# Two-layer retention and sparse-attention step: only real token rows move through the experts, splitting reordered, one weight unit's low half on Pool

## What is computed

```python
def grouped_moe(h, w_router, b_router, w_gate, w_up, w_down):
...
    vals, idx = lax.top_k(jnp.where(in_grp, probs, -jnp.inf), TOPK_EXPERTS)
    wts = vals / jnp.sum(vals, -1, keepdims=True)
    gates = jnp.sum(jax.nn.one_hot(idx, N_EXPERTS, dtype=F32) * wts[..., None], axis=-2).astype(h.dtype)
    y = jnp.zeros_like(h)
    for e in range(N_EXPERTS):
        a = jax.nn.silu(h @ w_gate[e]) * (h @ w_up[e])
        y = y + gates[..., e:e + 1] * (a @ w_down[e])
    return y
```

## Time and profile before

| | before |
|---|---|
| median of 3 runs | 2274.32 us (2268.29 to 2278.16) |
| the profiled execution's own time | 2277.34 us |
| span of its trace | 2275.6 us |
| PE busy | 1903.2 us (84%) |
| DVE busy | 1089.5 us (48%) |
| ACT busy | 768.7 us (34%) |
| POOL busy | 239.6 us (11%) |
| moved by DMA | 412.19 MB, mean 181 GB/s |

### The profile page before, as it was taken

How to read it: one execution, slowest core, us unless ns; L and a number is a source line. 1 busy time by engine, 2 the same in 40 slices (tenths; PEclk the granted TensorE clock), 3 DMA queues, 4 the chain that set the end, 5 groups by cost and what they waited for, 6 DMA issues and landing times.

```text
span 2275.6 us, 20410 instructions
## 1 busy us (share of the span) xinstructions
PE 1903.2 (84%) x6689; PEld 1039.8 (46%) x6689; DVE 1089.5 (48%) x1674; ACT 768.7 (34%) x993; POOL 239.6 (11%) x235
## 2 busy tenths in 40 slices
PE   2899899999899997399999479996568972999990
PEld 0443323343233334187878134343343441877870
DVE  0320352210342017298988371126742173989886
ACT  0110211111211001388786211124442021888861
POOL 0000000000000000432221120000000003122201
PEclk8899999999999997699999789995775975999995
DMA  9232172423163124699998922021002233999983
GB/s 340 102 133 77 72 277 75 158 75 111 67 247 105 54 74 147 244 359 392 392 393 332 378 77 79 20 58 38 1 1 74 85 140 102 367 393 392 393 301 122
DMA packets 194993, 412.19 MB, mean 181 GB/s; under 512 B 14382, under 2 KB 18558, under 8 KB 194877
## 3 DMA queue, kind: packets, MB, share of 16 engines
q1 hardware_dynamic: 168962, 322.26, 39.5%
q0 software_dynamic: 21248, 72.02, 8.4%
q10 hardware_dynamic: 4712, 17.02, 2.1%
HBM read 363.36 MB, written 47.90 MB: 181 GB/s over the span
## 4 chain that ended last, share of the span: by engine, by line
PE 68%; DVE 11%; DMA 8%; issue 4%; DVEq 4%; ACT 3%; POOL 1%; POOLq 0%; ACTq 0%; SPq 0%
PE bank L586 34%; PE bank L884 17%; PE bank L579 3%; DMA RING<-in_w_mod 3%; PE bank L811 3%; DMA RING<-in_w_gate 3%; ACT WH L1319 2%; PE bank L796 2%; PE bank L977 1%; PE bank L785 1%; DVEq L2228 1%; PE bank L664 1%; POOL slot_d L1644 1%; DVE WL L2083 1%; PE bank L781 1%
## 5 line engine op out<-in xcount | busy, mean ns | idle before, releaser
L586 PE MATMUL bank<-RING,HT 128*128 128x512 f32 (+3 forms) x1600 | 685.8, 584 | 15.9 <-ACT HT L1146 13.3
L2083 DVE TENSOR_TENSOR WL<-RING,WH 128x2048 fp32r<-128x2048 f32 x192 | 436.7, 2293 | 81.1 <-ACT WH L1319 79.4
L586 PEld LDWEIGHTS bank<-RING,HT 128*128 128x128 f32 (+1 forms) x1600 | 263.8, 172 | 397.8 <-issue 377.5
L1319 ACT ACTIVATE WH<-RING 128x2048 fp32r<-128x2048 f32 x192 | 364.9, 1915 | 115.4 <-PE bank L884 92.4
L579 PE MATMUL bank<-cst,M 128*128 128x128 f32 (+3 forms) x721 | 114.2, 289 | 119.4 <-DMA M<-h_d,slot_c 71.8
L884 PE MATMUL bank<-WH,HGH 128*128 128x512 f32 x512 | 204.1, 399 | 3.0 <-DVE HGL L2094 3.0
L884 PE MATMUL bank<-WL,HGH 128*128 128x512 f32 x512 | 201.3, 393 | 0.0
L884 PE MATMUL bank<-WH,HGL 128*128 128x512 f32 x512 | 201.3, 393 | 0.0
L579 PEld LDWEIGHTS bank<-cst,M 128*128 128x128 f32 (+3 forms) x721 | 92.0, 156 | 178.3 <-DMA M<-h_d,slot_c 72.8
L586 PE MATMUL bank<-RING,M 128*128 128x512 f32 (+1 forms) x320 | 138.6, 593 | 0.3 <-ACT M L1268 0.3
L884 PE MATMUL bank<-WH,ATH 128*128 128x512 f32 x256 | 102.8, 402 | 14.4 <-DVE ATL L2110 14.4
(11 more groups left out here) (277 smaller groups left out, 2095.1 us busy)
## 6 DMA issues: line engine op xcount, KB each, us to landing
RING<-in_w_gate SPq DMA_DIRECT2D x64, 1024.0 KB, 12.1
RING<-in_w_up SPq DMA_DIRECT2D x64, 1024.0 KB
RING<-in_w_down SPq DMA_DIRECT2D x64, 1024.0 KB, 12.0
RING<-in_w_mod SPq DMA_DIRECT2D x24, 2048.0 KB, 9.5
RING<-in_w_in_ret SPq DMA_DIRECT2D x12, 2048.0 KB, 12.1
RING<-in_state_ret SPq DMA_DIRECT2D x16, 1024.0 KB, 8.6
out_ret_sample<-RING POOLq DMA_DIRECT2D x16, 1024.0 KB, 6.8
RING<-in_w_in_dsa SPq DMA_DIRECT2D x5, 2048.0 KB, 14.4
```

The costliest lines, as they stand in the source:

```text
L586: last = pe.matmul(out, lhs[:, k, :], w[:, k, :], start=start and k == 0, stop=stop and k == K - 1)
L1319: act.activation(WH[:, u % SPLIT, :, :], raw(u % RAW), ACT.Copy).then_inc(S("hi_rdy"), 1)
L2083: TT(WL[:, u % SPLIT, :, :], raw(u % RAW), WH[:, u % SPLIT, :, :].bitcast(F32), ALU.subtract)\
```

## The change

Token rows alone move: the table of slots is filled with 1,040 (a row that doesn't exist) in place of 0, tokens are numbered 0 to 1,039 (k * 520 + token for a token's first and second expert), `h_d` holds the rows twice, and the gather skips rows out of range. The store of an item becomes an indirect DMA to `y_d`, by the same numbers, that skips rows out of range too. So `y_d` holds 1,040 rows in token order, and the end of a layer reads them with plain DMAs. The clearing of part of `y_d` at the start goes.

Another order of splitting: `take_a(1)` stands ahead of unit 12 on ACT and on DVE, and both halves of `take_y` are ACT's. The low half of unit 10 (POOL_UNIT, the eleventh of each pair) is POOL's; DVE waits for it at u = 10 and passes the count on to `lo_rdy` with a copy of one column.

The core of the diff:

```diff
@@ constants
-    tok[:, :] = (np.arange(TILES) * P)[None, :] + i[:, None]
+    tok[:, :, :] = (np.arange(2) * TOK)[None, :, None] + (np.arange(TILES) * P)[None, None, :] + i[:, None, None]
@@ scalar: pair(i, end)
                     def take_y(j, u):
                         used(u)
                         act.wait_ge(S(f"y_st{j}"), (i + 1) * 16)
-                        act.activation(Y[j][:, NB:D], bank[5 + 2 * j][:, :], ACT.Copy).then_inc(S(f"y_ev_a{j}"), 1)
+                        for h in range(2):
+                            act.activation(Y[j][:, h * NB:(h + 1) * NB], bank[4 + 2 * j + h][:, :], ACT.Copy)\
+                                .then_inc(S(f"y_ev{j}"), 1)
                     for u in range(SPLIT, SPLIT + len(UNITS)):
+                        if u == 12:
+                            take_a(1)
                         if not end or u < len(UNITS):
                             high(i, u)
...
-                        if u == 12:
-                            take_a(1)
@@ gpsimd
-            pool.dma_start(y_items[:, NE:, :],
-                           zero_f.rearrange("p (o d) -> p o d", o=1).to_broadcast([P, ITEMS - NE, D])).then_inc(S("y_zero"), 16)
-            pool.dma_start(slot_d.rearrange("(p i) o -> p (i o)", p=P), zero_i[:, :]).then_inc(S("slot_zero"), 16)
+            def no_slots():
+                pool.dma_start(slot_d.rearrange("(p i) o -> p (i o)", p=P), none_i[:, :]).then_inc(S("slot_zero"), 16)
+            no_slots()
@@ gpsimd: experts(l)
-                    pool.dma_start(h_d[cols(t), :], HN[t % 2][0:rows(t), :]).then_inc(S(f"h_st{t % 2}"), 16)
+                    pool.dma_start(h_d.rearrange("(k t) d -> t k d", k=2)[cols(t)],
+                                   HN[t % 2][0:rows(t), :].rearrange("p (o d) -> p o d", o=1).to_broadcast([rows(t), 2, D]))\
+                        .then_inc(S(f"h_st{t % 2}"), 16)
...
                 pool.wait_ge(S("slots_in"), 16 * (l + 1))
+                if l == 0:
+                    no_slots()
...
-                                            in_offset=bass.IndirectOffsetOnAxis(ap=slot_c[:, j:j + 1], axis=0))\
+                                            in_offset=bass.IndirectOffsetOnAxis(ap=slot_c[:, j:j + 1], axis=0),
+                                            bounds_check=2 * TOK - 1, oob_is_err=False)\
...
                 def store(j, k):
-                    pool.wait_ge(S(f"y_ev_d{j}"), (first + k) + 2)
-                    pool.wait_ge(S(f"y_ev_a{j}"), (first + k) + 2)
-                    pool.dma_start(y_items[:, bass.ds(k * 2 + j, 1), :].rearrange("p o d -> p (o d)"), Y[j][:, :])\
+                    pool.wait_ge(S(f"y_ev{j}"), (first + k) * 2 + 4)
+                    nc.gpsimd.tensor_tensor(slot_o[:, j:j + 1], slot_i[:, bass.ds(k * 2 + j, 1)], zero_i[:, 0:1], ALU.add)
+                    pool.drain()
+                    pool.indirect_dma_start(out=y_d, out_offset=bass.IndirectOffsetOnAxis(ap=slot_o[:, j:j + 1], axis=0),
+                                            in_=Y[j][:, :], in_offset=None, bounds_check=2 * TOK - 1, oob_is_err=False)\
                         .then_inc(S(f"y_st{j}"), 16)
+                def low(k):
+                    pool.wait_ge(S("hi_rdy"), (first + k) * len(UNITS) + (POOL_UNIT + 1))
+                    nc.gpsimd.tensor_tensor(WL[:, POOL_UNIT % SPLIT, :, :], raw(POOL_UNIT % RAW),
+                                            WH[:, POOL_UNIT % SPLIT, :, :].bitcast(F32), ALU.subtract)\
+                        .then_inc(S("pool_lo"), 1)
...
                     gather(1, k + 1)
+                    low(k)
                     store(0, k)
...
-                        pool.indirect_dma_start(out=YG[t % 2][k][0:R, :], out_offset=None, in_=y_d,
-                                                in_offset=bass.IndirectOffsetOnAxis(ap=dest_c[0:R, k, t:t + 1], axis=0))\
+                        pool.dma_start(YG[t % 2][k][0:R, :], y_d[k * TOK + t * P:k * TOK + t * P + R, :])\
@@ vector: pair(i, end)
+                        if u == 12:
+                            take_a(1)
+                        if u == POOL_UNIT:
+                            dve.wait_ge(S("pool_lo"), i + 1)
+                            dve.tensor_copy(nbias[:, 0:1], C("ones")[:, 0:1]).then_inc(S("lo_rdy"), 1)
-                        if not end or u < len(UNITS):
+                        elif not end or u < len(UNITS):
                             low(i, u)
...
-                        if u == 12:
-                            take_a(1)
-                        if u == 13:
-                            if not end:
-                                take_rows(0, i + 1)
-                            take_y(0, 9)
-                        if u == 15:
-                            take_y(1, 11)
+                        if u == 13 and not end:
+                            take_rows(0, i + 1)
```

More of the change, by code:

```diff
@@ L165, in trunk @@
         mod_d = dram("mod_d", (DEPTH, DEC + 1, 6 * D))
-        h_d = dram("h_d", (TOK, D))
+        h_d = dram("h_d", (2 * TOK, D))
         slot_d = dram("slot_d", (P * ITEMS, 1), I32)
-        y_d = dram("y_d", (P * ITEMS, D))
-        y_items = y_d.rearrange("(p i) d -> p i d", i=ITEMS)
+        y_d = dram("y_d", (2 * TOK, D))
         X = sb("X", [P, TILES, D])
@@ L184, in trunk @@
         rotc = sb("rotc", [P, 2, TILES, P])
-        tok = sb("tok", [P, TILES], I32)
+        tok = sb("tok", [P, 2, TILES], I32)
         zero_i = sb("zero_i", [P, ITEMS], I32)
+        none_i = sb("none_i", [P, ITEMS], I32)
         bf_cum = sb("bf_cum", [P, 2, P], BF16)
@@ L199, in trunk @@
         slot_c = sb("slot_c", [P, 2], I32)
-        dest_c = sb("dest_c", [P, 2, TILES], I32)
+        slot_o = sb("slot_o", [P, 2], I32)
         primer = sb("primer", [P, 2], I32)
@@ L280, in trunk @@
         UNIT0 = 8
+        POOL_UNIT = 10
         CROW = view(0, D, r=DEC + 1)
@@ L902, in pair @@
                     pe.wait_ge(S("hg_lo0"), 2 * (i + 1))
-                    pe.wait_ge(S("y_ev_d0"), i + 1)
+                    pe.wait_ge(S("y_ev0"), i * 2 + 1)
                     up(0, 0, 0)
                     turn_rows(1, i)
-                    pe.wait_ge(S("y_ev_a0"), i + 1)
+                    pe.wait_ge(S("y_ev0"), i * 2 + 2)
                     up(0, 1, 2)
                     pe.wait_ge(S("hg_lo1"), 2 * (i + 1))
-                    pe.wait_ge(S("y_ev_d1"), i + 1)
+                    pe.wait_ge(S("y_ev1"), i * 2 + 1)
                     up(1, 0, 4)
                     turn_a(0)
-                    pe.wait_ge(S("y_ev_a1"), i + 1)
+                    pe.wait_ge(S("y_ev1"), i * 2 + 2)
                     up(1, 1, 6)
@@ L1158, in _ @@
             for j in range(2):
-                act.nop().then_inc(S(f"y_ev_a{j}"), 1)
+                act.nop().then_inc(S(f"y_ev{j}"), 2)
             act.activation(CSIL[:, :], CROW[:, :], ACT.Silu).then_inc(S("c_silu"), 1)
@@ L1551, in _ @@
             for j in range(2):
[L1552 removed]
+                pool.dma_start(primer[j:j + 1, :], A["tok"][j:j + 1, 0, 0:2]).then_inc(S(f"y_st{j}"), 16)
             pool.dma_start(rotc[:, :, :, :], A["rotc"]).then_inc(S("const_in"), 16)
[L1554 removed]
+            pool.dma_start(tok[:, :, :], A["tok"]).then_inc(S("const_in"), 16)
             pool.dma_start(wr[:, :, :], A["w_router"].rearrange("(k p) e -> p k e", p=P)).then_inc(S("const_in"), 16)
@@ L1637, in experts @@
                         bias(g)
-                pool.wait_ge(S("slot_zero"), 16)
+                pool.wait_ge(S("slot_zero"), 16 * (l + 1))
                 pool.wait_ge(S("tables"), l + 1)
@@ L1678, in experts @@
                     gather(1, k + 1)
+                    low(k)
                     store(0, k)
                     store(1, k)
+                low(last)
                 store(0, last)
@@ L1685, in experts @@
                     pool.wait_ge(S(f"y_st{j}"), ((first + last) + 2) * 16)
-                nc.gpsimd.tensor_tensor(dest_c[:, :, :], dest_i[:, :, :],
-                                        zero_i[:, 0:2 * TILES].rearrange("p (k t) -> p k t", k=2), ALU.add)
-                pool.drain()
+                nc.gpsimd.tensor_tensor(slot_o[:, 0:1], slot_i[:, 0:1], zero_i[:, 0:1], ALU.add)
                 for t in range(TILES):
@@ L1786, in _ @@
             for j in range(2):
-                for name in ("a_rdy", "y_ev_d", "at_lo"):
+                for name in ("a_rdy", "at_lo"):
                     dve.engine_nop().then_inc(S(f"{name}{j}"), 1)
@@ L2111, in take_a @@
                            ATH[:, j, :, :].bitcast(F32), ALU.subtract).then_inc(S(f"at_lo{j}"), 1)
-                    def take_y(j, u):
-                        used(u)
-                        dve.wait_ge(S(f"y_st{j}"), (i + 1) * 16)
-                        dve.tensor_copy(Y[j][:, 0:NB], bank[4 + 2 * j][:, :]).then_inc(S(f"y_ev_d{j}"), 1)
                     for u in range(SPLIT, SPLIT + len(UNITS)):
```

8 lines of the change are left out of this document (3 added, 5 removed).

## The result

The changed kernel takes **2333.04 us** (median of 4 runs, 2324.8 to 2338.49), the kernel before, run beside it, 2275.91 us: a ratio of **1.0267** (95% interval 1.0245 to 1.0289). On the 2274.32 us of the forecast that is +60.7 us (55.7 to 65.7). The forecast was +27 us, 2301; the sign held, the size did not. The profiled execution is the shortest of the four: 2324.8 us, span 2322.2 us.

A forecast was written before the change was run, and what follows sets the result against it. PE was taken to bound the expert loop, with the DMA 0.8 us a pair away. Terms 38.4 - 14.4 - 2.5 + 3 + 3 + 0.6 - 1 = +27.1 us on 2274.32 gave 2301 us, range 2274 to 2335 us.

The forecast's parts named there:

- wait for POOL's part, started in time: At `turn_a(1)` PE waits 2.4 us per pair for `act_times_up`, behind POOL's 4.9 us low half: +38.4 us.
- POOL starts late: Only in layer 0's first pair, late gathers make POOL start the low half 3 us late: +3 us.
- lower clock behind the wait: In the expert loop, a lower granted clock after PE's wait; the forecast had no such term.
- all other terms together: `take_a(1)` order -14.4, rows -2.5, `take_y` on ACT +3, issue before the loop +0.6, end of layer 1 -1 us.
- the slack of 0.57 us: Before the change, `act_times_up` is done at 1096.05; PE needs it for `turn_a(1)` at 1096.62, when unit 8 ends.
- rival 2: POOL's low half takes T, its duration, up to 2.5 us and hides before unit 8 ends: 2260 us, chance 0.14.
- The end of the wait for ATL: With `take_a(1)` ahead of unit 12, PE's once-per-pair wait for ATL goes: -14.4 us.
- the DMA as second bound: Moving all rows and weights at 392 GB/s takes 37.4 us a pair, 0.8 us from PE's bound.
- the HGL wait: ACT's second `take_y` copy delays units 4, 5 and HGL: 0.2 us in 14 pairs, +3 us (0 to +8).
- no cost here, priced as a rival below: POOL's second gather is issued by 1093.9 as before, 0.8 us behind the high half, or sooner: no cost.
- rival 1: New stores' drains wait for landings; POOL's second gather ends late, 1.6 us in 12 pairs: +19, 2320 us, chance 0.19.

The follow-up runs named there:

- experiment 3: The changed kernel with POOL's low half of unit 10 put ahead of the second gather: 2300.04 us, ratio 1.0130 to the kernel before.
- experiment 8: The changed kernel with POOL's low half ahead of the second gather and the subtraction done twice on POOL: 2389.21 us, ratio 1.0512.
- experiment 9: The changed kernel with POOL's low half ahead of the second gather and 16 unused transposes in PE's wait before `turn_a(1)`: 2292.19 us, ratio 1.0092.
- experiment 1: The changed kernel with the low half of unit 10 given back to DVE, all else as changed: 2260.72 us, ratio 0.9954.
- experiment 11: The kernel before with only the moving of token rows alone added (slots, gathers, indirect stores, plain reads): 2270.97 us, ratio 0.9982.
- experiment 2: The kernel before with only POOL's low half of unit 10 and DVE's one-column copy added: 2324.74 us, ratio 1.0250.
- experiment 5: The changed kernel with POOL's low half ahead of the second gather and DVE's wait for it behind `act_times_up(1)` and `take_a(1)`: 2262.49 us, ratio 0.9959.

## Why the prediction went wrong

| term, us | forecast | measured | by |
|---|---|---|---|
| wait for POOL's part, started in time | 16 x 2.4 = 38.4 | 16.5 + 16.5 = 33.0 | experiment 3 |
| POOL starts late | 3 | 52.5 - 33.0 = 19.5 | waits after; experiment 3 |
| lower clock behind the wait | none | 16.0 | chain after; experiments 8, 9 |
| all other terms together | -14.3 | -10.5 (-14.5 to -6.4) | experiment 1 |
| sum | 27.1 | 58.0 | ratio: 60.7 (55.7 to 65.7) |

**Right.** The place (`act_times_up` behind POOL's low half, in every pair), the slack of 0.57 us and the step by step path to the wait. The Trainium skill's "GPSIMD Engine Reference", section "Performance versus the Vector engine", was nearer with its 4,497 ns than the 4.9 us taken from 3,072 columns on nine partitions; measured are 4,563 ns. The wait that the prediction estimated from the page's figure was 2.0 us, measured 2.05. The condition of rival 2 is confirmed too: at T = 2.4 the time is 2258 us, where the rival had 2260. The end of the wait for ATL, the DMA as second bound, and the HGL wait (2.9 and 3.0 us in the two layers where experiment 11, with `take_y` as before, has 1.5 in each: +2.9 us for a forecast of 3) came as worked out.

**The step that failed first: "no cost here, priced as a rival below".** The prediction took the second gather as issued by 1093.9 as before, 0.8 us behind the high half of unit 10, or a little sooner, and gave 3 us to the first pair of layer 0 alone. Two things were wrong with that.

First, `low` stands behind this gather in POOL's order, so by the prediction's own chain 0.8 us is a later start and a longer wait, some 11 us in 14 pairs. It was put at nothing without a reason. Experiment 2 shows it, with the old stores: waits of 2.8 to 3.7 us in twelve pairs, not 2.05.

Second, the gather does not stay where it was: with the new stores it comes 3.2 to 3.8 us behind the high half in experiment 1 and 6.0 to 8.7 in experiment 11. So the reason of rival 1, that each new store holds POOL's queue for a landing, holds. In the trace of the change 62 of the 64 gathers and stores of items, all but the first gather of each layer, are issued 0.83 to 1.05 us behind the later of two times: the end of their small copy and the landing of the DMA ahead. What stood against rival 1, half the bytes, did not help: the first and the second gather of a pair land in 8.5 and 7.1 us (medians in layer 0), before in 8.4 and 7.0.

In the change the first wait was 7.66 us, 5.6 over the base, five more are 0.4 to 4.5 over it, the other ten at most 0.15. That the sum of 19.5 us meets the 19 of rival 1 is luck, since its pattern was 1.6 us in twelve pairs. In program order `low` closes a ring through POOL's queue: store, gathers, `low`, PE, Y, the next store. PE's waits lengthen the pairs (39.5 to 42.6 us between second stores, about 36 in experiment 1), and this seems to give the queue time again: behind the wait of 5.39 us come one of 3.75 and one of 2.06.

**The step that was missing: the clock.** The sum priced a PE wait at its length. The kernel before had a clock of 1.00 in this loop, with waits of about 1 us a pair, so no row read there showed what a longer one does. It is 16.0 us in the profiled execution, the shortest of the four; the other three, with a mean granted clock of 0.890 to 0.893 over the span where this one has 0.896, are 7 to 14 us longer.

**Open.** In experiment 3 the clock fell in five of 16 pairs with equal waits, every third pair of a layer; why those is not settled. Nor is why just these six pairs of the change come late. Whether the drain or the indirect issue itself waits for the landing ahead is not shown either, since every indirect DMA of the loops has a drain ahead of it.

## What to carry to other kernels

Before you give a busy engine's work to an idle one, find the first instruction that stands behind the hand-over on the receiving and on the waiting engine: the same 4.6 us of POOL's work in each pair cost 70 us in one order and nothing in another (experiment 5). Give the helper work that is needed late, put it ahead of its slow DMA issues, and let the waiting engine do first what does not depend on it. And price a wait of TensorE at its length plus what the clock costs behind it.

## What the runs showed of the hardware

- Behind a wait of 2.05 us on TensorE, in a loop that else runs at a granted clock of 1.00, the clock was at 0.50 for a while in 5 of 16 pairs, and the 12 matmuls of unit 9 took 4.34 us instead of 2.74 (experiment 3). Behind a wait of 6.8 us all eight pairs of layer 0 lost 1.5 to 1.75 us (experiment 8). Sixteen transposes in the gap kept the clock at 1.00 (experiment 9).
- POOL's two-input subtraction from SBUF takes 4.5 to 4.6 us for 128 x 2,048 and 2.40 us for half of it, but 3.45 us when DVE runs a two-input subtraction of 1.23 us beside it.
- An indirect DMA of POOL with a small copy and a drain ahead was issued 0.83 to 1.05 us behind the later of that copy and the landing of the DMA ahead, in 62 of 64 cases. Gathers of half the rows landed no sooner (8.5 and 7.1 us, before 8.4 and 7.0).
